# Down projection of the later three FFNs: the first 16 inner tiles by seven block products

## The reference

```
x = x + 0.5 * ((silu(gate) * up) @ w_down)     gate, up = split(rmsnorm(x) @ w_up)     D_FF = 2816
x = x + mixer(rmsnorm(x))                      HGRN2, GLA and mLSTM branches, merged by gates
x = x + 0.5 * ((silu(gate) * up) @ w_down)     with other weights
```

## Time and profile before

| what | value |
|---|---|
| runs | 2972.44, 2976.24, 2976.67 us |
| span of the profiled execution, first to last instruction | 2971.1 us |
| TensorE busy | 2914.5 us, 98% |
| VectorE busy | 1610.6 us, 54% |
| GpSimd busy | 1600.8 us, 54% |
| ScalarE busy | 923.3 us, 31% |
| mean granted TensorE clock | 0.992 |
| moved by transfers | 444.36 MB, of it 125.83 MB by the sums of weights |

### The profile page before, as it was taken

The page is one execution under the profiler, slowest core; times in us unless marked ns, Lnnn a source line. Parts: engine busy times, 40 slices in busy tenths (PEclk is TensorE's granted clock), DMA queues, the critical chain, the costliest instruction groups (busy, mean ns, idle before and its releaser), DMA issues.

```text
span 2971.1 us, 60005 instructions
## 1 busy us (share of the span) xinstructions
PE 2914.5 (98%) x23308; PEld 2825.3 (95%) x23308; DVE 1610.6 (54%) x2325; ACT 923.3 (31%) x1551; POOL 1600.8 (54%) x1466
## 2 busy tenths in 40 slices
PE   8999999999999999999999999999999999999998
PEld 7999999989988899999999999999998889999998
DVE  8463775534332567473784737744453235783745
ACT  4121233031132325252452524321302323351423
POOL 6776676645553575425455254765555435744343
PEclk9999999999999999999999999999999999999999
DMA  5786859746521344453444533897364223443532
GB/s 201 191 260 192 212 177 279 181 151 157 136 79 51 118 141 138 128 166 114 128 142 131 162 114 106 239 243 209 111 168 119 65 69 106 154 154 117 173 116 85
DMA packets 196590, 444.36 MB, mean 150 GB/s; under 512 B 13272, under 2 KB 57184, under 8 KB 195552
## 3 DMA queue, kind: packets, MB, share of 16 engines
q1 hardware_dynamic: 106944, 280.08, 29.1%
q0 software_dynamic: 40128, 125.83, 17.6%
q10 hardware_dynamic: 49312, 35.59, 3.9%
HBM read 422.93 MB, written 144.35 MB: 191 GB/s over the span
## 4 chain that ended last, share of the span: by engine, by line
PE 89%; DVE 6%; ACT 1%; issue 1%; DMA 1%; PEld 1%; POOL 0%; ACTq 0%; DVEq 0%; SPq 0%; POOLq 0%
PE dense L677 54%; PE SA L737 14%; PE SB L737 10%; PE SA L875 1%; PE SA L960 1%; PE SA L861 1%; PE SA L944 1%; PE SA L804 1%; DVE tmp L1460 1%; DVE Hl L1465 1%; PE SB L956 1%; PE SA L947 1%; DMA raw<-wst 1%; PE SA L846 0%; PEld dense L677 0%
## 5 line engine op out<-in xcount | busy, mean ns | idle before, releaser
L547 POOL TENSOR_SCALAR Wh<-raw 128x512 fp32r<-128x512 f32 x620 | 455.7, 735 | 802.7 <-PEq L682 526.9
L549 POOL TENSOR_TENSOR Wl<-raw,Wh 128x512 fp32r<-128x512 f32 x620 | 853.4, 1376 | 51.8
L677 PE MATMUL dense<-Hh,Wh 128*128 128x272 f32 x2784 | 594.8, 295 | 21.3 <-DVE Hl L1451 9.3
L677 PE MATMUL dense<-Hh,Wl 128*128 128x272 f32 x2784 | 580.5, 290 | 0.0
L677 PE MATMUL dense<-Hl,Wh 128*128 128x272 f32 x2784 | 579.0, 290 | 0.0
L677 PEld LDWEIGHTS dense<-Hh,Wh 128*128 128x128 f32 x2784 | 441.4, 190 | 33.6 <-issue 15.9
L677 PEld LDWEIGHTS dense<-Hl,Wh 128*128 128x128 f32 x2784 | 442.0, 190 | 0.0
L677 PEld LDWEIGHTS dense<-Hh,Wl 128*128 128x128 f32 x2784 | 439.8, 191 | 0.0
L612 POOL TENSOR_TENSOR Sl<-pair,Sh 128x512 fp32r<-128x512 f32 x120 | 171.5, 1447 | 411.6 <-ACT Sh L1040 410.8
L677 PE MATMUL dense<-Ah,Wh 128*128 128x272 f32 x1408 | 291.1, 288 | 1.0 <-POOLq L551 0.9
L677 PE MATMUL dense<-Ah,Wl 128*128 128x272 f32 x1408 | 289.5, 288 | 0.0
(11 more groups left out here) (452 smaller groups left out, 6359.6 us busy)
## 6 DMA issues: line engine op xcount, KB each, us to landing
raw<-wst SPq DMA_DIRECT2D x276, 512.0 KB, 3.6
w_sums<-wst POOLq DMA_DIRECT2D x36, 1536.0 KB, 13.3
w_sums<-wst POOLq DMA_DIRECT2D x18, 2048.0 KB, 16.1
pair<-wst SPq DMA_DIRECT2D x120, 256.0 KB, 3.5
pair<-w_sums SPq DMA_DIRECT2D x60, 512.0 KB, 3.7
wsum<-w_sums SPq DMA_DIRECT2D x60, 512.0 KB, 3.6
w_sums<-w_sums POOLq DMA_DIRECT2D x12, 1536.0 KB, 12.3
wsum<-wst SPq DMA_DIRECT2D x60, 256.0 KB, 2.6
```

The lines of the kernel that those rows point to most:

```text
L547: pool.tensor_scalar(Wh[:, j, cs], raw[:, j, cs], 1.0, 0.0, ALU.mult, ALU.add).then_inc(glink, 1)
L549: pool.tensor_tensor(Wl[:, j, cs], raw[:, j, cs], f32(Wh[:, j, cs]), ALU.subtract).then_inc(glink, 1)
L677: mm = pe.matmul(dps[slot][:, a, 0:HALF], w[:, ring, w0:w0 + 128], x[:, k, a * HALF:(a + 1) * HALF], start=(k == 0 and n == 0), stop=(k == ...
```

## The change

In f = 1, 2 and 3, the down projection of inner tiles 0 to 15 also goes by seven block products. A block of 8 hidden tiles (two inner halves of 4) and two output tiles make one `fast` step, so that each block of 8 has 4 such steps, and they replace 8 tiles of `dense` each. The hidden tiles 16 to 21 go through `dense` as before.

- The steps of an FFN are one list, `STEPS`, written out without loops: up 0 to 6, down 0 to 3, up 7 to 14, down 4 to 7, up 15 to 19.
- The hidden tiles of a block are made in the order 0, 4, 1, 5, 2, 6, 3, 7 (`HIDDEN`), since a block sum needs a tile of each inner half.
- Each such pair of hidden tiles gets four sums, of 128x272 each, by GpSimd (`mixed_sums`); ScalarE makes the high parts of the four in one instruction (`mixed_hi`), VectorE the low parts in one (`mixed_part_lo`).
- The sums of the down weights are made by 8 more transfers for each block of 4 steps, issued by GpSimd: for f = 1 and 3 in the mixer before, for f = 2 within f = 1 (`down_sums`).
- The raw down weights of inner tiles 0 to 15 are no longer loaded and split by GpSimd.
- VectorE adds the combined products to `X` by block halves (`down_products`).

```diff
+HIDDEN = [b * FF_BLOCK + p // 2 + p % 2 * (FF_BLOCK // 2) for b in range(2) for p in range(FF_BLOCK)]
+STEPS = [("up", i) for i in range(FAST_AT[1] + 1)] + [("down", o) for o in range(DOWN_PAIRS)]
+STEPS += [("up", i) for i in range(FAST_AT[1] + 1, FAST_AT[2] + 1)]
+STEPS += [("down", DOWN_PAIRS + o) for o in range(DOWN_PAIRS)]
+STEPS += [("up", i) for i in range(FAST_AT[2] + 1, FAST)]
+LATE = (FAST_AT[1], FAST_AT[2])
...
+            def mixed_sums(f, which, hp):
+                if hp:
+                    pool.wait_ge(pair_mid, (UP0[f] + 2 * hp - 1) * 3 + 3)
...
+                E, O, T = tmp[:, 0, :], tmp[:, 1, :], mixed[which]
+                pool.tensor_tensor(T[:, 0, :], E[:, h0], E[:, h1], ALU.subtract).then_inc(mix_sum, 1)
+                pool.tensor_tensor(T[:, 1, :], E[:, h1], O[:, h1], ALU.subtract).then_inc(mix_sum, 1)
+                pool.wait_ge(mix_sum, 4 * n + 1)
+                pool.tensor_tensor(T[:, 3, :], T[:, 0, :], O[:, h1], ALU.add).then_inc(mix_sum, 1)
+                pool.wait_ge(mix_sum, 4 * n + 3)
+                pool.tensor_tensor(T[:, 2, :], T[:, 3, :], O[:, h0], ALU.subtract).then_inc(mix_sum, 1)
...  GpSimd, order of an FFN
-                for b, nf in enumerate((FF_BLOCK, FF_BLOCK, FF_LAST)):
-                    one(p0 + DOWN_AT[0][b], nf * P)
-                    for i in range(FAST_AT[b] + 1, min(FAST_AT[b + 1] + 1, FAST)):
-                        lows(f, i)
-                    for m in range(1, KT):
-                        one(p0 + DOWN_AT[0][b] + m, nf * P)
+                for s, (what, i) in enumerate(STEPS):
+                    if what == "up" and i % 2 == 0 and i <= LATE[1]:
+                        mixed_sums(f, which, i // 2)
+                    if s + 1 < PAIRS:
+                        lows(f, s + 1)
+                    if f == 1 and s < 16:
+                        down_sums(2, s)
+                    if s >= PAIRS - 3:
+                        one(p0 + DOWN_AT[0][2] + s - (PAIRS - 3), FF_LAST * P)
...  TensorE
-                        with pe.Fori(FAST_AT[b], FAST_AT[b + 1]) as i:
-                            fast(i)
+                        for s, (what, i) in enumerate(STEPS):
+                            if what == "up":
+                                fast(s, normed)
+                                continue
+                            if i % DOWN_PAIRS == 0:
+                                pe.wait_ge(mix_lo, HID_PAIRS * (f - 1) + (i // DOWN_PAIRS + 1) * HID_PAIRS // 2)
+                                pe.sem_inc(step_began, 1)
+                            fast(s, hidden_part)
...  ScalarE, up step: after the silu
+                    if j == 0 and i <= LATE[1]:
+                        mixed_hi(i // 2)
+                    ahead(s, A22)
...  VectorE, up step: after the hidden tile
+                    ahead(s, A22)
+                    if j == 0 and i <= LATE[1]:
+                        mixed_part_lo(i // 2)
+                    if i not in LATE:
+                        hidden_part_lo(i + 2)
...  VectorE, down step: after product 2, 4, 5, 5, 6, 6, 6, 7, 7, with the lows between them as before
+                    TT(U[:, h1], SA[:, 1, h0], U[:, h0], ALU.subtract).then_inc(prod_read, 1)
+                    STT(X[:, m, h0], SA[:, 0, h0], 0.5, X[:, m, h0], ALU.mult, ALU.add).then_inc(prod_read, 1)
+                    TT(V, SA[:, 1, h0], U[:, h0], ALU.subtract).then_inc(prod_read, 1)
+                    TT(D, V, D, ALU.subtract).then_inc(down_mid, 1)
+                    TT(W, SB[:, 0, h0], U[:, h1], ALU.subtract).then_inc(prod_read, 1)
+                    STT(X[:, m + 1, h1], D, 0.5, X[:, m + 1, h1], ALU.mult, ALU.add).then_inc(down_x, 1)
+                    STT(X[:, m, h1], W, 0.5, X[:, m, h1], ALU.mult, ALU.add).then_inc(down_x, 1)
+                    TT(E, V, SB[:, 1, h0], ALU.subtract).then_inc(prod_read, 1)
+                    STT(X[:, m + 1, h0], E, 0.5, X[:, m + 1, h0], ALU.mult, ALU.add).then_inc(down_x, 1)
```

More of the change, by code:

```diff
@@ L358, in build @@
         sum_three = sem("sum_three")
+        sum_down = [sem(f"sum_down{c}") for c in range(2)]
+        sum_down3 = sem("sum_down3")
+        mix_sum, mix_hi, mix_lo = sem("mix_sum"), sem("mix_hi"), sem("mix_lo")
+        down_mid, down_x = sem("down_mid"), sem("down_x")
         q_lo_pool = sem("q_lo_pool")
@@ L638, in ffn @@
             def ffn(f, p0):
+                which = f % 2
                 for t in range(4):
@@ L708, in ffn, with normed, hidden_part @@
                 alternate = f == 0
-                def fast(i):
+                h0, h1 = slice(0, HALF), slice(HALF, TOK)
+                def normed(q, k):
+                    if q in (A11, A12, S4):
+                        at, h = {A11: (k, h0), A12: (4 + k, h0), S4: (4 + k, h1)}[q]
+                        return hi[:, at, h], lo[:, at, h]
+                    j = {S1: 0, S2: 3, S3: 1, A22: 2}[q]
+                    return Th[which][:, k, j, :], Tl[which][:, k, j, :]
+                def hidden_part(q, k):
+                    if q in (A11, A12, S4):
+                        j = {A11: 0, A12: 1, S4: 2}[q]
+                        return PH[k][:, j, :], PL[k][:, j, :]
+                    j = {S1: 0, S2: 3, S3: 1, A22: 2}[q]
+                    return QH[k][:, j, :], mixed_lo(which, k)[:, j, :]
@@ L754, in ffn @@
                                 up(UP_AT[b] + j, i)
-                            fast(HALF_AT[b] + i)
-                    else:
-                        with pe.Fori(FAST_AT[b], FAST_AT[b + 1]) as i:
-                            fast(i)
+                            fast(HALF_AT[b] + i, normed)
+                    elif b == 0:
+                        for s, (what, i) in enumerate(STEPS):
+                            if what == "up":
+                                fast(s, normed)
[4 more added lines that the diff above has]
+                            fast(s, hidden_part)
+                    if b < 2 and not alternate:
+                        continue
                     hidden = L * (2 * FF_TILES) + (which * FF_TILES + b * FF_BLOCK)
@@ new lines, in up_products, with down_products @@
+                    if i not in LATE:
+                        hidden_hi(i + 2)
+                def down_products(s, d):
+                    n, e = PAIR0[f] + s, 2 * DOWN_PAIRS * (f - 1) + d
+                    act.wait_ge(prod_read, n * 5 + 3)
+                    act.wait_ge(prod_done, 7 + n * 7 + 1)
+                    act.activation(tmp[:, 3, 0:HALF], SA[:, 0, 0:HALF], ACT.Copy).then_inc(prod_copy, 1)
+                    ahead(s, A11, S2)
+                    if e:
+                        act.wait_ge(down_x, 3 * e - 2)
+                    act.wait_ge(prod_done, 7 + n * 7 + 3)
+                    act.activation(tmp[:, 5, HALF:TOK], SB[:, 0, 0:HALF], ACT.Copy).then_inc(prod_copy, 1)
+                    ahead(s, S1, A12, S3, S4, A22)
@@ L1618, in products @@
                     TT(V[:, h1], V[:, h0], V[:, h1], ALU.subtract).then_inc(pair_mid, 1)
[L1619 to L1620 removed]
+                    ahead(s, S3)
                     product(n, 6)
```

342 lines of the change are left out of this document (232 added, 110 removed).

## The result

| | before | after |
|---|---|---|
| median of the runs beside each other | 2976.45 us (2972.44 to 2980.42, 4 runs) | 3013.57 us (3010.00 to 3016.49, 4 runs) |
| span of the profiled execution | 2971.1 us | 3014.6 us |
| mean granted clock | 0.992 | 0.984 |
| moved | 444.36 MB | 520.50 MB |

The ratio is 1.0127, 95% interval 1.0114 to 1.0140: slower by 37 us. The forecast was 3020 (2962 to 3055), with 0.75 on slower. The profiled execution of after is the longest of its four runs (3016.49 us), and that of before, by its span, is near the short end of its own, so the two spans lie 43.5 us apart and the medians 37.

The account below looks back on a forecast made before the run. The prediction took TensorE's matmul issue to bound the FFNs. Its terms, -34.8 + 42 + 25 + 3.6 + 7.8 = +43.6 us on a 2971.1 us span, plus 5.1 to the median, gave 3020 us (2962 to 3055).

Parts of the forecast that it names:

- The step from span to median: Conversion of the forecast span into a median of runs: 5.1 us added, the distance seen in the kernel before.
- What is saved: Six down groups on TensorE: 4 fast steps replace 8 dense tiles, 33.9 us, plus a 0.9 us stall gone; -34.8 us.
- The wait before a down group: TensorE stalls before six down groups for VectorE's low parts of the fourth pair's sums: 7.0 each, 42 us.
- Odd up steps: Odd up steps behind a pair's sums run late, four at 1.9 and one at 0.8 per FFN: 25 us.
- The first round: Odd up step: ScalarE's copy of the first product 0.55 us late, then 0.3 more before S3.
- second round: GpSimd's lows in the odd step hand on late, which comes back in the following pair: about 1.0 us.
- Last steps: Last three steps of an FFN: GpSimd's down weight splits run beside VectorE's late part; 1.2 us an FFN, 3.6 us.
- The clock: A half-clock stretch on TensorE after each of six long stalls: 1.3 us lost each, 7.8 us.
- The new adding transfers: 16 more issues by GpSimd for each of 3 FFNs, moving 50 MB: nothing, at worst 5 us.
- The rule of shared access: Of VectorE and GpSimd operations with both inputs in SBUF only one runs; the second waits for the whole other.
- Keep up except at the wait: Rival: sums fit into gaps and only a 4.1 us stall before down groups remains; 2974 us, chance 0.18.
- VectorE as the bound of every up step: Rival: late lows also delay loads, so a pair of up steps costs 5 us; 3070 us, chance 0.13.

Follow-up runs that it names:

- e1: After, with high and low parts of the fourth pair's sums made half a step earlier, before each down group: 2974.72 us, ratio 0.9996.
- e2: After, with GpSimd's four sums replaced by constant fills that read nothing, so the output isn't the FFN's: 2988.21 us, ratio 1.0050.
- e9: After, with the edits of e1 and e3 together: 2963.61 us, ratio 0.9960.
- e8: After, with the edits of e1, e3 and e5, and a pair's third and fourth sum made behind GpSimd's next lows: 2969.42 us, ratio 0.9984.
- b1: The kernel before, with only its first chunk of weight sums grown from six tiles to seven: 2982.50 us, ratio 1.0023.
- e3: After, with the 24 older sum transfers of a mixer issued at every second weight piece: 3001.14 us, ratio 1.0084.
- e5: After, with ScalarE copying the odd up step's first product ahead of the hidden tile's high part: 3022.80 us, ratio 1.0165.
- e4: e1, with TensorE's wait for the last sums moved behind the down products that don't need them: 2974.80 us, ratio 1.0002.
- e10: e9, with a pair's third and fourth sum made after GpSimd's lows for the next step, except before a down group: 2959.23 us, ratio 0.9939.
- e11: e9, with low parts of the other pairs' sums moved into VectorE's former idle gap in the odd step: 2974.10 us, ratio 0.9997.
- b2: The kernel before, with its own weight sum transfers issued at every second step of a mixer, as in e3: 2971.42 us, ratio 0.9981.

## Why the prediction was right, and where its sum was not

The sign, the mechanism and the range held; 3020 forecast against 3013.6. On the profiled spans the agreement is closer than it deserves: +43.6 forecast, +43.5 measured, with errors that cancel: the odd steps and the last ones were put 15 us too high, and the mixers' 13.5 us were left out. The step from span to median failed: it added 5.1 us, the distance in before, and in after the median (3013.57) is 1 us under the span of the profiled execution (3014.6). So 43.5 us between the spans are 37 between the medians.

- **What is saved, 34.8 us.** Right. The 288 matmuls are gone, down steps behind the first are 10.55 apart to 0.03, and e1's three FFNs come out at +26.2 (14.0 + 11.9 + 0.3) - 34.8 = -8.6, measured -7.8.
- **The wait before a down group, 42 us.** Right in place, releaser and size: 6.3 us of waiting each, 37.7 in all, and with what precedes it 39.5 for the six steps. The working holds too: silu was put at 11.95 into the step and starts at 12.37 (2864.18 - 2851.81), the low parts were to end at 16.3 and end at 16.7. The step in the trace began with VectorE already late, which the 0.5 to 1 us for leftovers stood for. e2 gives the undisturbed stall that was worked out as 4.1: 4.2 at the lowest.
- **Odd up steps, 25 us.** Right in mechanism, twice too large: 13.1 us for all up steps, of it 1.7 in two even ones. Four odd steps of an FFN were put at 1.9 and one at 0.8. The trace has 1.0 to 1.2 for i = 5, 11 and 13, 0.4 for i = 3, and 0.2 to 0.5 for i = 9. The first round, 0.55 at the copy and 0.3 at U, is there: at the copy TensorE loses up to 0.8 and before S3 0.1 to 0.2, which the view of waits doesn't list. Kernel after, step i = 5 of f = 3, U and the first matmul of S3:

```profile
2709.61 0.43 DVE L1796 TENSOR_TENSOR tmp<-SA,tmp 128x272 f32<-128x272 f32 x1
...
2710.19 0.37 PE L857 MATMUL SA<-ThH,Sh 128*128 128x272 f32 x1
```

The term that was too large is the second round of about 1.0 from GpSimd's late lows, which no odd step shows; and i = 3 lost next to nothing.
- **Last steps, 3.6 us.** Measured 0.7.
- **The clock, 7.8 us.** Measured 10.9. I had taken the nearer row, after 2.31 us; the stalls here are 6.3, followed by 2.9 to 5.4 us at half speed, and 1.3 to 2.5 us were lost each, 1.8 on average, between the 1.3 and the 3.3 that the two stretches gave.
- **The new adding transfers, nothing (up to 5).** With the even order, the 16 new ones in each mixer cost little (both mixers together +1.0 in e9, up to +5.6 in e8), and the 16 in f = 1 seem to cost some 3 us. The bytes were put too low: 76 MB more are moved (444.36 to 520.50), not 50, since a down step also loads seven blocks in place of four. What I missed is that the old ones grow: the group's boundary moved by one tile, the first group's transfers from 1536 to 1792 KB, and where the issues are bunched (steps 1, 3, 4, 6, 7 and so on) GpSimd waits for the landing and its splits come late. The diff shows it (`FAST_AT[1] + 1`), and I had weighed only the added issues. Worth 13.5 us in the profiled execution, 6.8 (b1) to 12 (e3) by the medians.
- **The rule of shared access.** The earlier trace rows and the Trainium skill ("SBUF — State Buffer", on the two separate sides) said that one engine waits for the whole instruction of the other. The traces agree: 1.52 for 0.43 in e5, 2.38 for 1.28 in e4, and 0.73 undisturbed beside e2's fills, which read nothing. How much of the up steps' 13 us is the blocking alone is not separated by e2, whose fills are shorter too. The advice of the same page of the Trainium skill, in its rules for kernel authors, to schedule the one that is off the critical path is what e10 does, for 7.6 us in the up steps (14.2 to 6.6).
- **The rivals.** "Keep up except at the wait" is not what happened, but what e1 comes to when the wait is moved: 2974.7, its 2974 by another road. That the two times agree is chance: e1 still has 14 us of stretched up steps and 11 in the mixers, and a shorter wait. "VectorE as the bound of every up step" fell: even steps are 10.6.

So against the 34.8 us saved, the placing of one pair of instructions costs 39, the grown sum some 7 to 12, and the four sums 13 in the up steps besides what they add to the wait. With the first two gone and the third halved (e10) the change is worth having.

What stays open: the 1.7 us before each group in e10, 10 us in all, which e4 moved but didn't remove; whether the late weights of f = 1 come from the adding transfers there; and why the mixers' stretches at half clock lie elsewhere from kernel to kernel with the same matmuls there (by the clock records of the traces 6 of 34 us in before, 9 of 41 in after, 10 of 51 in e4). This makes a mixer's time in one execution uncertain by some us, as e4's +16.2 shows.

## What to carry to other kernels

When a seemingly free engine is given new work, place it instruction by instruction in the busiest step of the engine that shares its memory side, and put the urgent half first: the same four sums cost 14 us in one order and 7 in another. Read idle time again after each edit; a gap of the kernel before may be gone. A wait before a group is priced by where the awaited instruction stands in its engine's list, so look for the earliest place that its inputs allow before judging the algorithm. And when a diff shifts a boundary by one, look at every transfer whose size hangs on it, not only at the transfers that were added.

## What was new about the hardware

- After stalls of 6.3 us (after) and 4.2 to 5.1 us (e2) the first down step lost 1.8 us each on average at the half clock (10.9 and 11.3 over six); after stalls of 1.6 to 1.8 us (e1, e9, e10) nothing, 0.2 to 0.3 over six. Shortening the stalls from 6.3 to 4.2 saved nothing of the clock's part; to 1.7 all of it.
- A difference of 0.3 us in the order of two engines decides over 1.1 us: VectorE's low part of 128x272 takes 0.43 when it starts 0.14 ahead of a low of GpSimd's (after) and 1.52 when it starts 0.14 behind (e5).
- VectorE's idle 1.42 us of the earlier trace rows was gone in e9, where the low ahead of it takes 1.43 for 0.68; 1.3 us of work placed there (e11) cost 10 us.
- The transfers that make the sums, copying and adding ones together, land 16.8 us after their issue at 2048 KB, 15.8 at 1792 and 13.0 at 1536 (medians, the page after, its list of issues). By the program's semaphore the next one of the same sum waits for the landing: GpSimd waits 4.4 us in all in before, 6.4 with a quarter of a megabyte more in the first group (b1), 12.4 in after, and nothing with the issues spread evenly (b2, e3).
